# Attention's input product in 24 steps of seven products, x taken half by half

## The reference, cut to what matters

```
h = x @ w_in                                   # 1024 x 3088: q 512, k 512, v 1024, g 1024, lr 16
gk = log_sigmoid(lr @ w_gk + b_gk) / 16
bcum = cumsum of gk inside a chunk of 64 rows
qe, ke, kd = q * exp(bcum), k * exp(-bcum), k * exp(b_last - bcum)
... chunked attention with qe, ke, kd, v ...   # the stage attend
o = rms_norm(o) * norm_w * silu(g);  x1 = layernorm(alpha * x + o @ w_out)
... pooling mixer: x1 @ pool_w_in, windows of 2, 4, 8, 16 rows, per-group product, silu gate, @ pool_w_out
```

## Time and profile before

| | |
|---|---|
| three runs, median | 2002.89 us (2000.88 to 2003.55) |
| the profiled execution, its own time | 2001.48 us |
| its span, first to last instruction | 1999.6 us |
| prepare, last matmul starts at | 131.93 us |
| project, first and last matmul | 135.29 and 690.27 us |
| attend, first matmul | 692.81 us |
| last stage, first product | some 1042 us |
| PE busy, by the page | 96% of the span |
| DVE, ACT, POOL busy | 58%, 35%, 22% |

### The profile page before, as it was taken

One profiled execution on the slowest core, in us unless ns is written; L12 is line 12 of the kernel. 1 busy time (PEld: TensorE's weight loads), 2 busy tenths in 40 slices (PEclk: granted clock), 3 DMA queues, 4 the chain that ended last, 5 costly groups with the idle time before them and its releaser, 6 DMA issues.

```text
span 1999.6 us, 24456 instructions
## 1 busy us (share of the span) xinstructions
PE 1914.5 (96%) x8974; PEld 1588.5 (79%) x8974; DVE 1161.7 (58%) x1539; ACT 701.3 (35%) x1065; POOL 431.5 (22%) x268
## 2 busy tenths in 40 slices
PE   8999999999999989999949999999999999999997
PEld 7778887888888778888738888887888886787786
DVE  4330102332415277787675688868678657546998
ACT  4441213131313243343354444344434335224331
POOL 0005200000000000000043666423334343322430
PEclk9999999999999999999979999999999999999999
DMA  8766530334233464455322444333322225647342
GB/s 254 221 202 239 178 103 17 108 87 118 79 101 87 159 242 164 172 187 170 136 96 74 153 141 152 135 104 137 129 88 73 94 74 193 249 170 272 129 177 95
DMA packets 229912, 287.74 MB, mean 144 GB/s; under 512 B 17216, under 2 KB 170176, under 8 KB 227904
## 3 DMA queue, kind: packets, MB, share of 16 engines
q1 hardware_dynamic: 225216, 278.20, 42.0%
q10 hardware_dynamic: 4608, 8.39, 1.1%
HBM read 186.93 MB, written 99.61 MB: 143 GB/s over the span
## 4 chain that ended last, share of the span: by engine, by line
PE 41%; DVE 4%; issue 4%; ACT 1%; POOL 0%; DVEq 0%; POOLq 0%; ACTq 0%
PE banks L165 13%; PE banks L166 13%; PE banks L167 13%; DVE m_w_lo L1922 1%; DVE m_x_lo L1936 1%; ACT m_x_hi L1728 0%; DVE m_x_lo L1914 0%; PE banks L1621 0%; PE banks L1668 0%; DVE m_stats L2025 0%; DVE m_x_lo L1896 0%; DVE m_res L2019 0%; DVE m_res L2035 0%; POOL m_s L1859 0%; DVE m_win_b L1968 0%
## 5 line engine op out<-in xcount | busy, mean ns | idle before, releaser
L165 PE MATMUL banks<-m_x_hi,m_w_hi 128*128 128x512 f32 x1320 | 517.6, 392 | 9.4 <-DVE m_res L2019 3.5
L166 PE MATMUL banks<-m_x_lo,m_w_hi 128*128 128x512 f32 x1320 | 515.3, 390 | 0.0
L167 PE MATMUL banks<-m_x_hi,m_w_lo 128*128 128x512 f32 x1320 | 515.0, 390 | 0.0
L165 PEld LDWEIGHTS banks<-m_x_hi,m_w_hi 128*128 128x128 f32 x1320 | 248.7, 188 | 63.7 <-DVE m_w_lo L1922 10.0
L166 PEld LDWEIGHTS banks<-m_x_lo,m_w_hi 128*128 128x128 f32 x1320 | 248.8, 188 | 52.0 <-issue 0.7
L167 PEld LDWEIGHTS banks<-m_x_hi,m_w_lo 128*128 128x128 f32 x1320 | 248.7, 188 | 52.0
L1854 POOL TENSOR_TENSOR m_s<-pair_raw 128x512 f32<-128x512 f32 x24 | 47.3, 1969 | 891.6 <-POOLq L947 757.5
L165 PE MATMUL banks<-x_hi,h_w_hi 128*128 128x512 f32 x512 | 199.9, 390 | 0.8 <-DVE h_g_out L833 0.8
L166 PE MATMUL banks<-x_lo,h_w_hi 128*128 128x512 f32 x512 | 199.3, 389 | 0.0
L167 PE MATMUL banks<-x_hi,h_w_lo 128*128 128x512 f32 x512 | 199.3, 389 | 0.0
L1716 ACT ACTIVATE m_w_hi<-m_s 128x512 fp32r<-128x512 f32 x184 | 115.5, 629 | 202.7 <-PE banks L167 179.2
(11 more groups left out here) (220 smaller groups left out, 3117.7 us busy)
## 6 DMA issues: line engine op xcount, KB each, us to landing
p_in<-in_pool_w_in SPq DMA_DIRECT2D x32, 256.0 KB, 4.9
p_rows<-in_x SPq DMA_DIRECT2D x16, 512.0 KB, 5.2
w_fused<-p_out SPq DMA_DIRECT2D x32, 256.0 KB, 3.9
...
w_terms<-h_out_terms SPq DMA_DIRECT2D x8, 1024.0 KB, 5.6
...
```

Source lines behind the costliest of these rows:

```text
L165: nc.tensor.matmul(out, a_hi, b_hi, start=first, stop=False, skip_group_check=True)
L166: nc.tensor.matmul(out, a_hi, b_lo, start=False, stop=False, skip_group_check=True)
L167: return nc.tensor.matmul(out, a_lo, b_hi, start=False, stop=last, skip_group_check=True)
```

## The change

What it does:

- **prepare** turns and stores only the first 8 of 16 row tiles of x, now as they are (no split), in DRAM (x_in). It loads the four blocks of the v columns (1 MB each, in tiles 10, 12, 14 and 16), POOL makes three differences of them and one more (16 operations of 128x512, once all four blocks have landed), and ACT and DVE split all seven (b_hi, b_lo), 14 parts of 128x1024, one per tile from tile 18 on (`FIRST_PART`).
- **project** runs 24 steps of seven products of 12 matmuls. Steps 0 to 7 make v: the v weights move, a pair of row tiles of x is stationary. Steps 8 to 15 make g, q, k for the first half of x, 16 to 23 for the second: x moves, weights are stationary, and b_hi, b_lo are overwritten with x's seven blocks of 1 MB each (`load_x`, `turn_hi`, `turn_lo`) during steps 7 and 8, and 15 and 16. The other 8 row tiles of x are turned in steps 0 to 3. POOL makes the sums of the stationary side in all steps, DVE those of x (`x_terms`). The gates' first factor takes 2 x 40 matmuls.
- q, k and the gates are made per head and half, by tables that say after which product of which step a piece stands (`Q_AT`, `KEYS_AT`, `TURN_KEYS_AT`, ...).
- `load_qkv` is issued at the very end of the stage, behind the last store of g.
- The sums of pool_w_out move from project to steps 17 to 26 of the last stage.

The diff, cut to its core:

```diff
@@ prepare
+    V_LOADS = {1: (0, 0), 7: (0, BLK), 3: (HALF_K, BLK), 2: (HALF_K, 0)}
+    V_LOADS_AT = {10: 1, 12: 7, 14: 3, 16: 2}
+    FIRST_PART = 18
+    PAIR_AT = 26
-            return n // 2 if n % 2 else None
+            return n // 4 if n % 4 == 1 else None
+                    if n in V_LOADS_AT:
+                        load_values(V_LOADS_AT[n])
...
+                for j in V_LOADS:
+                    pool.wait_ge(b_loaded[j], DMA)
+                for k in range(HALF_K):
+                    at = 4 * k
+                    nc.gpsimd.tensor_tensor(p.b_raw[5][:, k, :], b12[:, k, :], b11[:, k, :], ALU.subtract
+                                            ).then_inc(b_summed, 1)
...
                     if n >= 1:
                         copy_out(n - 1)
+                    if n >= FIRST_PART:
+                        act.wait_ge(b_summed, 4 * HALF_K)
+                        j, rows = ORDER[(n - FIRST_PART) // 2], slice((n - FIRST_PART) % 2 * 2, (n - FIRST_PART) % 2 * 2 + 2)
+                        nc.scalar.activation(p.b_hi[j][:, rows, :], p.b_raw[j][:, rows, :], ACT.Copy).then_inc(b_hi_done, 1)
@@ project
+    V_STEPS = NT // 2
+    EPOCH = V_STEPS
+    STEPS = 3 * EPOCH
+    UNITS = (("g", 0), ("g", 1), ("qk", 0), ("qk", 1), ("g", 2), ("qk", 2), ("qk", 3), ("g", 3))
+    Q_AT = {0: (3, -1), 1: (4, 4), 2: (6, 0), 3: (7, 4)}
+    KEYS_AT = {0: ((3, 1), (3, 0)), 1: ((4, 5), (5, -1)), 2: ((6, 2), (6, 1)), 3: ((7, 5), (8, -1))}
+    TURN_KEYS_AT = {0: (3, 3), 1: (5, 0), 2: (6, 4), 3: (8, 0)}
+    TURN_LO = {0: (0, 4), 1: (0, 5), 2: (1, -1), 3: (1, 0), 4: (1, 1), 5: (1, 2), 6: (1, 3)}
...
+            def product(i, n):
+                j = ORDER[n]
+                pe.wait_ge(w_lo_done, PRODUCTS * i + n + 1)
+                if i and i % EPOCH == 0:
+                    pe.wait_ge(x_lo_done, turns_to(i // EPOCH, n))
...
+                for k in range(HALF_K):
+                    last = split_product(nc, shaped(i, bank(i, j)), w_hi[j][:, k, :], w_lo[j][:, k, :],
+                                         moving(i, x_hi[j], k), moving(i, x_lo[j], k), opens and k == 0, k == HALF_K - 1)
...
+            def turn_keys(m):
+
+                for n in range(2):
+                    pe.wait_ge(k_done[n], m + 1)
...
+            for i in range(STEPS):
+                for n in range(PRODUCTS):
+                    product(i, n)
...
+                    for m in due(TURN_KEYS_AT, i, n):
+                        turn_keys(m)
...
+            turn_keys(2 * HEADS - 1)
...
+            store_k(2 * HEADS - 1, 1)
+            store_kn(2 * HEADS - 1)
+            store_gates(2 * HEADS - 1)
...
+            for s in range(2):
+                p.load_qkv(sp, s, s)
@@ pool_mix_and_out
+    OUT_CHUNKS, FIRST_OUT_CHUNK = 2 * HALF_K, MT + 1
+                if 0 <= i - FIRST_OUT_CHUNK - 1 < OUT_CHUNKS:
+                    out_sums(i - FIRST_OUT_CHUNK - 1)
```

1176 lines of the change are left out of this document (756 added, 420 removed).

## The result

| | before | changed |
|---|---|---|
| median | 2003.22 us | 2049.43 us |
| lowest to highest of 4 runs | 2000.88 to 2004.32 | 2047.83 to 2050.62 |
| ratio | | 1.0232, 95% interval [1.0214, 1.0249] |
| span of the profiled execution | 1999.6 us | 2046.1 us |
| mean granted clock | 0.985 | 0.964 |

A forecast was written before the change was run, and what follows sets the result against it. PE, busy 96% of the span, was taken as the bound. -63.8 (matmuls) + 19.5 (prepare) + 17 (project) + 16.5 (project's end, cold restart) + 1 (last stage) = -9.8 us, from 2002.9 to 1993; range 1971 to 2015.

The forecast's parts named there:

- the price of project's 24 steps: Project: DVE late at four places (keys, two replacements of x's blocks, everything else), +17 us in all.
- The PE work that goes, -63.8: Whole kernel: 288 fewer matmuls save 65.3 us; with added matmuls and vanished short waits, -63.8 us together.
- Prepare, +19.5 (12.9 with x gone): Prepare: ACT's wait for POOL's sums stalls PE, net +14.5; later tiles with x +4.0, delayed p_in +1; +19.5 us together.
- Keys of steps 13 and 21, "+2 each": Project, steps 13 and 21: head 1's second keys come late on DVE for PE's turn, +2 us each, +4 together.
- Steps 7 to 8, "+3": Project: x's first half replaces the v blocks, DVE's rests and additions pile up, +3 us (bounds 0 and 8).
- Steps 15 to 16, "+8": Project: second replacement with queries and head 3's keys ahead on DVE; PE stands 8.2 us, +8 (bounds 3 and 16).
- Everything else in 24 steps: +2: Project: all losses outside the key steps and the two replacements, +2 us over 24 steps.
- Colder clock, "+1 cold": Attention's start: a colder PE at the restart after project's end, +1 us.
- The end of project, T + 17.7: Attention begins 17.7 us after T, the end of project's last product, against 2.15 today: +15.5 (bounds 11 and 20).
- The last stage, "+1 (bounds 0 and 10)": Last stage, steps 17 to 26: POOL's 32 added sums of pool_w_out mostly hide in its slack, +1 us.
- the rule of mutual exclusion: Project's replacements: two-SBUF-input DVE and SBUF-reading POOL instructions exclude each other; in full, the sum comes some 10 us higher.
- DVE becomes the bound: Rival, project steps 12, 15, 16, 20, 23: DVE's work beside POOL stretches, +25 us, 2018 us; chance 0.2.

The follow-up runs named there:

- e5_small_weight_sums: Changed kernel with POOL's four weight sums of project's steps 1 to 23 made on 8 elements a partition in place of 512, data wrong: 2028.3 us, ratio 1.0122.
- e1_early_v: Changed kernel with prepare's four v blocks issued at tiles 2, 4, 6 and 8 in place of 10, 12, 14 and 16: 2034.8 us, ratio 1.0155.
- e12_out_sums_on_dve: Changed kernel with the last stage's 32 sums of pool_w_out made by DVE at the end of steps 18 to 25, not by POOL: 2033.7 us, ratio 1.0157.
- the best version: Changed kernel with early v blocks, reordered rows, terms, keys and stores, later key turns, and most weight sums and all pool_w_out sums on DVE: 1999.7 us, ratio 0.9978.

## Why the prediction was wrong, point by point

The step that failed is the price of project's 24 steps. It was +17 above PE's own work, and the runs show 57. Four places were priced, "everything else" was +2 (measured some 18), and nothing was put down for the colder clock between them or for what POOL's sums cost (17 by e5_small_weight_sums). The same omission made the last stage +1 in place of 15.

- **The PE work that goes, -63.8.** Right as far as the intervals show it. Steps 4 to 6 stand 19.04 apart, steps 1 to 3 with their x turns 20.8.
- **Prepare, +19.5 (12.9 with x gone).** Right: 15.1. The last block landed after 7.1 (8 forecast), the sums took 20.5 (20.6), PE's stall was 15.38 behind a wait of 3.03, 18.4 together (18.7); e1_early_v shows the cause. The later tiles with x lost 1.2 each in three waits, as forecast (+4.0). One row was misread: the 4.2 us that the stall was to cover are not tile 20's wait but the kernel's very first load. At tile 20 the kernel before waits 0.78, and 0.61 and 1.56 behind it, 2.95 in all, so some 1.2 too much was taken off. Two rows of the kernel before:

```profile
4.19 1.09 PE L302 MATMUL banks<-ident,p_in 128*128 128x128 f32 x4 [4.19 <-DMA p_in<-in_pool_w_in]
...
80.46 0.66 PE L302 MATMUL banks<-ident,p_in 128*128 128x128 f32 x4 [0.78 <-DMA p_in<-in_pool_w_in]
```

- **Keys of steps 13 and 21, "+2 each".** Mis-sized: 6.8 and 8.3 above the 20.4 that the matmuls and the turn take. PE's wait for the keys was 2.45, for 2 forecast, but PE also waited for the seed of the next step (2.15), which was not priced; the rest, some 2 us and more, has no row of its own. In the step before each an addition was late as well (1.52).
- **Steps 7 to 8, "+3".** 5.6; inside the bounds of 0 and 8.
- **Steps 15 to 16, "+8".** The wait for the keys was 8.37, as forecast; the place lost 19.3 (67.8 less 48.5), outside its bounds of 3 and 16. Missed were four more waits of PE (2.27, 0.40, 2.30 and 1.31, together 6.3), one of them behind ACT's wait for the store of kn, and the clock (0.85 on average in step 16).
- **"Everything else in 24 steps: +2".** Failed: some 18. Step 0 alone lost 9.3, by two waits that I never priced: SP loads the second tile of rows behind a load that waits for DVE, and DVE stands until a single buffer is stored. Both are plain in the new code; I costed DVE's durations and not what is queued behind its waits.
- **Colder clock, "+1 cold" at the restart of attention only.** Failed. Between project's first seed and last product PE's listed waits are some 43 us and the loss is 57. The other 14 I put down to matmuls at a lower granted clock (0.78 in 520:540, where the earlier trace rows stood at full speed); that is a remainder, not a row. In the last stage the same: a wait of 3.00 in step 22 made its interval 23.9, 4.9 over, at a mean granted clock of 0.93.
- **The end of project, T + 17.7.** Right: 18.2, from 705.28 to 723.45.
- **The last stage, "+1 (bounds 0 and 10)".** The worst step for its size: 15. I asked whether POOL had time for its sums (it had: 96 us of 144) and not what they do to DVE. The runs put that at 33 us of DVE in seven steps and 15.7 us of time (e12_out_sums_on_dve), although showed POOL's own stretching, and I had weighed the rule of mutual exclusion, but only at project's two replacements.
- **Rivals.** "DVE becomes the bound" (2018) was nearest by its number, not by its places. Steps 12 and 20 took 20.8 us with DVE busy for 15.3, step 15 25.8 with 18.5, step 16 42.0 with 25.0, and step 23 lost nothing: there PE stood for DVE's, ACT's and SP's order and not for a full DVE. DVE was nearly full beside POOL in the last stage, which this rival left out.
- **The sum of the misses.** 39 in project, 14 in the last stage, 2 in prepare, 1 in attention: 56, the distance from 1993 to 2049. In project they are roughly 11 at the keys of steps 13 and 21, 3 at steps 7 to 8, 11 at steps 15 to 16 and 16 in the other steps.

What stays open: the 11.5 us (60.0 less 48.5) that steps 15 and 16 lose in the best version too, why steps without an edit differ from profile to profile (step 8 33.5 to 36.5 us with the same code, step 0 30.1 to 32.6), and whether a second buffer of x rows would remove the rest in steps 0 and 1, which was not tried.
